# mLSTM heads of block 1: another form of the norm, gate rows spread by a transfer, and the output product cut into pieces between the heads

## What is computed

```python
att = moba_attention(q_a, k_a, v_a)                      # 8 heads of 64, causal
m_t = jnp.maximum(m_inter, jnp.max(d, axis=-1))          # mLSTM, 4 heads, q and k 64 wide, v 128
s = jnp.einsum('bhtd,bhsd->bhts', qc, kc) * jnp.exp(d - m_t[..., None])
...
h = num / jnp.maximum(jnp.abs(den), jnp.exp(-m_t))[..., None]
...
hm = hm * lax.rsqrt(jnp.mean(hm * hm, axis=-1, keepdims=True) + EPS)
hm = hm.transpose(0, 2, 1, 3).reshape(B, S, ML_V_W) * g_mlstm_out.astype(jnp.float32)
hm = hm * jax.nn.sigmoid(mo.astype(jnp.float32))
mixed = jnp.concatenate([att, hm], axis=-1).astype(x.dtype)
x = x + rms_norm(mixed @ w_out, g_mix_post)
```

## Time and profile before

| | us |
|---|---|
| median of 3 runs | 1155.46 (1154.97 to 1156.65) |
| time of the profiled execution | 1161.27 |
| its span in the trace | 1159.4 |
| TensorE busy | 1118.0 (96%) |
| VectorE busy | 816.5 (70%) |
| ScalarE busy | 526.2 (45%) |

### The profile page before, as it was taken

How to read it: one execution, slowest core, us unless ns; L and a number is a source line. 1 busy time by engine, 2 the same in 40 slices (tenths; PEclk the granted TensorE clock), 3 DMA queues, 4 the chain that set the end, 5 groups by cost and what they waited for, 6 DMA issues and landing times.

```text
span 1159.4 us, 19626 instructions
## 1 busy us (share of the span) xinstructions
PE 1118.0 (96%) x8440; PEld 1055.6 (91%) x8440; DVE 816.5 (70%) x1090; ACT 526.2 (45%) x605; POOL 12.0 (1%) x26
## 2 busy tenths in 40 slices
PE   6999888999999899999999999999999999999998
PEld 5878677999999798988999999999899899999998
DVE  5865576776766599885787788768989377666442
ACT  4544444656333543553653444345355455444432
POOL 4000000000000000000000000000000000000000
PEclk9999889999999999999998999999999999999998
DMA  7533323878887164424778998965443275676540
GB/s 211 182 121 135 108 79 105 326 267 297 315 285 252 38 218 153 138 74 158 259 257 288 319 313 294 326 213 168 166 146 110 82 261 183 204 252 202 179 165 37
DMA packets 131494, 228.61 MB, mean 197 GB/s; under 512 B 5925, under 2 KB 59539, under 8 KB 131409
## 3 DMA queue, kind: packets, MB, share of 16 engines
q1 hardware_dynamic: 130404, 227.11, 58.1%
q0 software_dynamic: 672, 0.06, 0.1%
q10 hardware_dynamic: 333, 0.21, 0.1%
HBM read 226.30 MB, written 1.05 MB: 196 GB/s over the span
## 4 chain that ended last, share of the span: by engine, by line
PE 73%; DVE 17%; ACT 6%; issue 2%; DMA 2%; SPq 0%; DVEq 0%; ACTq 0%
PE mm L422 62%; DVE lo L1117 5%; DVE cacc L1197 4%; ACT hi L799 3%; PE mm L461 2%; PE pv L479 2%; DMA raw<-in_w_out_dram 1%; PE pa L506 1%; DVE ada_acc L1138 1%; DVE sB L1205 1%; PE pv L521 1%; PE pa L501 1%; PE pv L706 1%; DMA raw<-in_w_ffn_in_dram 1%; DVE pB L1496 1%
## 5 line engine op out<-in xcount | busy, mean ns | idle before, releaser
L422 PE MATMUL mm<-act_hi,hi 128*128 128x256 f32 x1760 | 493.0, 284 | 6.0 <-ACT act_hi L861 2.7
L422 PE MATMUL mm<-act_hi,lo 128*128 128x256 f32 x1760 | 486.6, 280 | 0.0
L1117 DVE TENSOR_TENSOR lo<-raw,hi 128x2048 fp32r<-128x2048 f32 (+1 forms) x160 | 361.9, 2265 | 173.6 <-ACT hi L799 172.2
L422 PE MATMUL mm<-act_lo,hi 128*128 128x256 f32 x1760 | 470.1, 280 | 0.0
L799 ACT ACTIVATE hi<-raw 128x2048 fp32r<-128x2048 f32 (+1 forms) x160 | 301.5, 1889 | 226.7 <-PE mm L422 180.5
L422 PEld LDWEIGHTS mm<-act_hi,hi 128*128 128x128 f32 x1760 | 332.5, 189 | 11.8 <-issue 9.5
L422 PEld LDWEIGHTS mm<-act_hi,lo 128*128 128x128 f32 x1760 | 332.9, 189 | 0.8 <-issue 0.7
L422 PEld LDWEIGHTS mm<-act_lo,hi 128*128 128x128 f32 x1760 | 322.4, 189 | 0.0
L422 PE MATMUL mm<-u_hi,hi 128*128 128x256 f32 x608 | 170.7, 281 | 0.0
L422 PE MATMUL mm<-u_lo,hi 128*128 128x256 f32 x608 | 170.4, 280 | 0.0
L422 PE MATMUL mm<-u_hi,lo 128*128 128x256 f32 x608 | 169.2, 278 | 0.0
(11 more groups left out here) (247 smaller groups left out, 995.1 us busy)
## 6 DMA issues: line engine op xcount, KB each, us to landing
ada_raw<-in_ada_w_dram SPq DMA_DIRECT2D x96, 512.0 KB, 6.0
raw<-in_w_ffn_in_dram SPq DMA_DIRECT2D x88, 512.0 KB, 6.0
raw<-in_w_in_dram SPq DMA_DIRECT2D x40, 1024.0 KB, 5.1
raw<-in_w_ffn_out_dram SPq DMA_DIRECT2D x20, 1024.0 KB, 6.0
raw<-in_w_up_dram SPq DMA_DIRECT2D x16, 1024.0 KB, 6.6
raw<-in_w_down_dram SPq DMA_DIRECT2D x16, 1024.0 KB, 7.8
raw<-in_w_out_dram SPq DMA_DIRECT2D x12, 1024.0 KB, 5.1
raw<-in_w_in_dram SPq DMA_DIRECT2D x16, 512.0 KB, 5.3
```

The source lines that it names most:

```text
L422: ins = pe.matmul(o, w[:, kk, fs], a[:, k, :], start=(k == 0 and i == 0 and f % 2 == 0), stop=(ends and i == len(pairs) - 1), skip_group_c ...
L1117: v(dve.tensor_tensor(lo[:, c % RING, 0:nk, :], raw[:, c % RING, 0:nk, :], hi[:, c % RING, 0:nk, :].bitcast(F32), ALU.subtract), "lo_done")
```

## The change

It has these parts:

- `gate_rows` limits the row of the exponent to at most 41. The rows are then written to a buffer in DRAM by one transfer that ScalarE issues in unit 1, and read back, with 128 copies of each row, by four that it issues in unit 2. `bcA` has room for four heads. The spreading product L626 and the copy L934 go.
- The mask is added (0 or -1e30) before the exponential, in the instructions of `m_args`; the multiplication with the mask (L1355) goes. There are buffers `sM` and `pM` of the heads' own.
- The division goes. The norm of numerator/d equals numerator · (mean(numerator²) + eps · d²)^-1/2. ScalarE squares numerator and denominator and copies the numerator (`m_sums_out`); `emA` is exp(2·row); VectorE takes the larger of the two squares (`m_larger`) and adds eps·128 times it to the sum of squares (`m_total`); ScalarE makes the root from that (`m_root`).
- The transposes of the gates go to unit 3, the arguments of heads 0 and 1 to units 5 and 6, and unit 8, which only drained, is written out.
- The output product is cut by input tile, 12 matmuls a piece (`out_pieces`), and the pieces stand between the last units and the heads.
- ScalarE loads the table with exp and tanh after the softplus and the one with ln at the first root.

```diff
@@ TensorE
-            for i in range(UNITS + 1):
+            for i in range(UNITS):
...
                 if i + 1 < UNITS:
                     scores(qk1, i + 1)
-                if i < UNITS:
-                    turn(pA[:, i % 2, :])
+                else:
+                    out_pieces(0, (0, 1))
+                    for g in (3, 4):
+                        pe.wait_ge(sem(freed(("in", g))[0]), freed(("in", g))[1])
+                    m_scores(0)
+                turn(pA[:, i % 2, :])
...
-                full(pe.matmul(bank(1)[:], ident[0:4, h:h + 1].to_broadcast([4, P]), gate[:, 2:4, :], start=True, stop=True), 1)
...
-            m_scores(0)
-            for h in range(MH + 1):
+            out_pieces(1, (0,))
+            u = UNITS - 1
+            apply_v(ptA[:, u % 2, :], v1, u * QK, QK, QK * (u % 2), True)
+            out_pieces(0, (2,))
+            for h, (half, ks) in enumerate(((1, (1,)), (0, (3,)), (1, (2,)), (1, (3,)))):
+                m_sums(h)
                 if h + 1 < MH:
                     m_scores(h + 1)
-                if h < MH:
-                    m_sums(h)
-                if h in fill_at:
-                    chunk(("out", fill_at[h]), 0, att_hi, att_lo, ready=None if fill_at[h] else "act_ready")
-                if h:
-                    head_squares()
-
-            for half in range(2):
-                chunk(("out", half), 1, act_hi, act_lo, ready=None if half else "act_ready")
+                out_pieces(half, ks)
+                head_squares()
+                squares_at.append(filled.seen("a"))
+            out_pieces(0, (4, 5, 6, 7))
+            chunk(("out", 1), 1, act_hi, act_lo)
@@ ScalarE
+            def m_exps(h):
+
+                wait("mexp_arg_ready")
+                a(act.activation(sM[:, h % 2, :], sM[:, h % 2, :], ACT.Exp))
+                a(act.activation(emA[:, h % 2, :], bcA[:, h, S:2 * S], ACT.Exp, scale=2.0), "mexp_done")
+
+            def m_sums_out(h):
...
+                a(act.activation(sq[:, 0, :], b[:, 0:S], ACT.Square), "hsq_ready")
+                a(act.activation(bcA[:, h, 0:S], b[:, S:2 * S], ACT.Square), "den_ready")
+                if h >= 2:
+                    act.wait_ge(sem("of_ready"), MH + h - 1)
+                a(act.activation(hmA[:, h % 2, :], b[:, 0:S], ACT.Copy), "bank2_free", sums_at[h])
+
+            def m_root(h):
+
+                log_tables()
+                wait("head_sum_ready")
...
+                if i == 1:
+                    wait("gate_rows_ready")
+                    act.dma_start(gate_rows_dram[:, :], gate[:, 2:4, :].rearrange("h r s -> h (r s)")).then_inc(sem("gates_out"), 16)
+                if i == 2:
+                    act.wait_ge(sem("gates_out"), 16)
+                    for h in range(MH):
+                        act.dma_start(bcA[:, h, :], gate_rows_dram[h].partition_broadcast(P)).then_inc(sem("gates_spread"), 16)
...
+            for h in range(MH):
+                m_sums_out(h)
+                if h:
+                    m_high(h - 1)
+                m_root(h)
+                if h + 2 < MH:
+                    m_exps(h + 2)
+                if h == 2:
+                    split(groups[("out", 1)][1][0] + LEAD)
@@ VectorE
+            def m_args(h):
...
+                dve.wait_ge(sem("gates_spread"), 16 * MH)
+                v(dve.scalar_tensor_tensor(out=sM[:, i, 0:S], in0=b[:, 0:S], scalar=acol[:, 0, h:h + 1], in1=cst[:, C_UP:C_UP + S],
+                                           op0=ALU.add, op1=ALU.add))
...
-                link(dve.tensor_tensor(d, b[:, S:2 * S], emA[:, i, :], ALU.max))
-                link(dve.scalar_tensor_tensor(out=d, in0=b[:, S:2 * S], scalar=-1.0, in1=d, op0=ALU.mult, op1=ALU.max))
-                link(dve.reciprocal(d, d))
-                link(dve.tensor_tensor(hmA[:, i, :], b[:, 0:S], d, ALU.mult), "bank2_free")
...
+            for h in range(MH):
+                m_larger(h)
+                if h + 1 < MH:
+                    m_weights(h + 1)
+                if h:
+                    m_final(h - 1)
+                m_total(h)
+                if h:
+                    m_low(h - 1)
+                if h + 2 < MH:
+                    m_args(h + 2)
+            m_final(MH - 1)
+            m_low(MH - 1)
+            split(groups[("out", 1)][1][0] + LEAD)
```

More of the change, by code:

```diff
@@ L87, in constants @@
     c[:, C_ADD + 2 * P:C_ADD + 3 * P] = tri
[L88 to L91, removed]
+    up = np.where(i[:, None] <= i[None, :], 0.0, -1e30)
+    c[:, C_UP:C_UP + P] = up
+    c[:, C_UP + 2 * P:C_UP + 3 * P] = up
     return c
@@ L642, in m_sums, with out_pieces @@
                 full(pe.matmul(b[:, S + P:2 * S], ones, w[:, S:3 * P], start=False, stop=True, skip_group_check=True), 2)
-            m_scores(0)
-            for h in range(MH + 1):
+                sums_at.append(filled.seen(2))
+            def out_pieces(half, ks):
+                name = ("out", half)
+                g, ids = groups[name]
+                for k in ks:
+                    j, kk = divmod(k, CK)
+                    if kk == 0:
+                        begin(name, j)
+                    if half == 0:
+                        wait("act_ready")
+                    ins = tile_products(2 * (g % 2), ids[j] % RING, kk, k, range(GT), ((att_hi, att_lo), (act_hi, act_lo))[j], k == KD - 1)
+                    if kk == CK - 1:
+                        ins.then_inc(sem("mm_done"), 1)
@@ new lines, in _ @@
+            for i in range(UNITS):
+                if i < len(todoA):
+                    name, j = todoA[i]
+                    chunk(name, j, act_hi, act_lo, token_major=name in (("in", 2), ("in", 4)))
+                if i + 1 < UNITS:
+                    scores(qk1, i + 1)
+                else:
[4 more added lines that the diff above has]
+                turn(pA[:, i % 2, :])
+                u = i - 1
+                if u == 0:
+                    pe.wait_ge(sem(freed(("in", 2))[0]), freed(("in", 2))[1])
+                if u >= 0:
+                    apply_v(ptA[:, u % 2, :], v1, u * QK, QK, QK * (u % 2), u % 2 == 1)
+                if i == 3:
+                    wait("gate_rows_ready")
+                    b = bank(0)
+                    for tt in range(TT):
+                        ins = pe.transpose(b[:, 4 * tt:4 * tt + 4], gate[:, 5, tt * P:tt * P + P], ident[0:4, 0:4])
+                    full(ins, 0)
@@ new lines, in m_weights, with m_larger @@
+            def m_weights(h):
+                i = h % 2
+                wait("mexp_done")
+                link(dve.scalar_tensor_tensor(out=pM[:, i, :], in0=full(0)[:, 0:3 * P], scalar=SCALE, in1=sM[:, i, :],
+                                              op0=ALU.mult, op1=ALU.mult), "bank0_free")
+                dve.sem_inc(sem("mweights_ready"), 1)
+            def m_larger(h):
+                i = h % 2
+                wait("den_ready")
+                link(dve.tensor_tensor(emA[:, i, :], emA[:, i, :], bcA[:, h, 0:S], ALU.max))
@@ L1328, in _, with m_low, take_heads @@
+            def m_low(h):
+                low(hf[:, h % 2, :], act_hi[:, 4 + h, :], act_lo[:, 4 + h, :], "act_hi_ready", "act_ready")
+                v.settle()
+            def take_heads(h):
+                v(dve.tensor_copy(hf[:, h % 2, :], full(2)[:, 0:S]), "bank2_free")
+                v.settle()
+                dve.sem_inc(sem("of_ready"), 1)
+            for i in range(UNITS):
+                probs(i, pA)
                 if i == 0:
@@ L1334, in _ @@
                     softmax_max(i + 1, sA)
+                if i == 3:
+                    link(dve.tensor_copy(acol[:].rearrange("p t h -> p (t h)"), full(0)[:, 0:8]), "bank0_free")
                 if i % 2 == 1 and i >= 3:
                     low_of_heads(i // 2 - 1)
+                if i == 5:
+                    m_args(0)
+                if i == 6:
+                    m_args(1)
                 if i >= 2 and i % 2 == 0:
[L1338 to L1339 removed]
@@ L1382, in _ @@
-            m_args(0)
-            m_weights(0)
-            for h in range(MH + 1):
-                if h in fill_at:
-                    split(groups[("out", fill_at[h])][1][0] + LEAD)
+                    take_heads(i // 2 - 1)
+            m_weights(0)
+            take_heads(MH - 1)
+            split(groups[("out", 0)][1][0] + LEAD)
+            low_of_heads(MH - 1)
+            for h in range(MH):
+                m_larger(h)
                 if h + 1 < MH:
-                    m_args(h + 1)
```

139 lines of the change are left out of this document (53 added, 86 removed).

## The result

The changed kernel takes **1141.32 us** (median of 4 runs, 1138.15 to 1143.9); the kernel before, timed beside it, takes 1155.22 (4 runs, 1154.02 to 1156.65). The ratio is 0.9887, with a 95% interval of 0.9867 to 0.9908: faster by 13.9 us, where 13.8 was forecast. A second pair, taken later, gave 1140.65 beside 1156.46, ratio 0.9868 [0.9854, 0.9883], 15.8 us.

The account below looks back on a forecast made before the run. TensorE bounds the rest (954.07 of 969.90 us busy); waits and slow clock cost the stage. 115.7 + 39.9 + 5.4 = 161.0 (walk 161.2) against 175.01; 13.8 off the 1155.46 median gives 1141.7 us, range 1137.0 to 1148.0.

Parts of the forecast that it names:

- The forecast point: Start of the norm's sums of squares on TensorE: 161.2 us by the walk, against 175.01 before, 13.8 less.
- the stage: The stretch the change touches, from the end of the last input chunk to the norm; 59.55 us before.
- the 115.7: End of the attention units' input chunks, where the changed stretch starts: 115.7 us, 0.25 later than before.
- its sign of being right: Norm's sums of squares starting at 160 to 163 us of the trace, among other signs such as clock mostly 1.00.
- TensorE's work: TensorE's instructions in the changed stretch at full clock, without waits: 39.9 us; four removed spreading products 4.5 us.
- The waits: TensorE waiting for head 3, its squares, its piece, the last chunk and the norm: 0.9, 1.6, 0.7, 0.8, 1.4 us.
- the handovers of 0.1 us: Assumed delay when one engine releases another: about 0.1 us; 0 or 0.15 each moves the walk by 0.8.
- The 0.25 us: Later end of the units, from gate transposes in unit 3 waiting for VectorE: 0.25 us, bounds 0 and 1.4.
- the near bound: Landing time for the spread gate rows' transfers: 5.0 us for 1 MB; the far bound was 11.6 for 384.5 KB.
- Rival 3: Spread rows land late, VectorE waits in unit 5; about 5 us slack, then one for one, up to 1161.5; 5%.
- Rival 1: Clock still falls in part of the changed stretch, costing 1 to 6 us: 1143 to 1148, say 1145; 16%.
- The table load: ScalarE's ln table load before head 0's root: 1.28 us by the trace; the skill's 2.66 would save 0.2 less.

Follow-up runs that it names:

- the repeat: The changed kernel run once more, nothing altered: 1140.65 us beside 1156.46 for the kernel before, ratio 0.9868.
- The early split: Changed kernel with ScalarE's `hi` and VectorE's `lo` of the output product's fourth chunk made earlier, the addition before the norm not moved: 1137.03 us, ratio 0.9845.
- whole chunks: Changed kernel with the first half of the output product in two whole chunks instead of pieces: 1145.79 us, ratio 0.9921.
- the late spread: Changed kernel with the four transfers that spread the gate rows issued in unit 5 instead of unit 2: 1143.85 us, ratio 0.9895.

## Why the prediction was right

**The forecast point.** 161.2 was forecast, 160.40 came. Two errors stand behind this that partly cancel: the stage starts 1.0 later than the 115.7 taken, which the repeat shows to be no effect of the change (115.08 there), and it takes 43.7 instead of 45.5. In the repeat the point is at 158.76, outside the 160 to 163 that the prediction gave as its sign of being right, so meeting it here to 0.8 was in part luck.

**TensorE's work.** 43.68 less the four marked waits of 4.03 is 39.65, against 39.9. Its parts were less exact. A turn takes 4.20 instead of 4.59: sums 1.40 instead of 1.66 and squares 0.43 instead of 0.63, while a piece costs 1.52 and not 1.45. The sums and squares were read from a place of the earlier trace rows where they followed and preceded other instructions, and a distance to the next start belongs to both neighbours. Over the stage the differences cancel; nobody should count on that. The spreading products were taken at 1.12, the length of one, where the distance to the next instruction is 1.05: 4.2 us for the four and not 4.5. The forecast point doesn't rest on this.

**The waits.** Forecast 0.9, 1.6, 0.7, 0.8 and 1.4, together 5.4. Found in the same places and with the same releasers 0.68, 1.41, about 0.3 (a gap at 150.87 that the trace doesn't mark as a wait), 0.66 and 1.28. Each is a little smaller, so the answers came a little earlier than by the handovers of 0.1 us; which handover was too long I haven't sorted out. This is the term that was mis-sized, by 1.4 us with the unmarked gap left out. The early split confirms the reading of two of them: with the `hi` gone from ahead of the last squares, the 1.41 goes.

**Ahead of the stage.** The 0.25 us came, but not as the wait that was forecast: from the scores of unit 1 to those of unit 7, the last, it is 46.80 us, where it was 46.59 before, and the transposes in unit 3 take 0.22 with no wait in front of them. The spread rows cost nothing, as taken. A transfer of 256 KB landed in 6.2 us, where the near bound was 5.0 for 1 MB, and the four had some 16 us to spare (95 to 111). They are copies out of 8 KB, not out of 16 as the prediction says, and the four issues took 1.8 us of ScalarE's queue and not 1.3. Rival 3 was priced rightly: the slack is 5.2 where 5 was said, but beyond it the cost was not one for one in the traced execution: 2.25 us of waiting cost 5.09, with the clock (3.2 by the medians).

**The clock.** Rival 1 didn't come in the change. It came in the trace of each experiment that took the dense pieces away or made the waits longer: whole chunks, the division back, the late spread. That it was a live risk and not a remote one is shown by the two executions that part at 121.24.

**The table load.** ScalarE waited until 132.80 for VectorE, longer than a load of 1.28 from 130.35 asks. By the 2.66 us that the Trainium skill (ScalarE: Activation LUTs, What ACT_TABLE_LOAD costs) gives for a switch, it could not have gone on before 133.01; here it went on 2.45 after the load's start. With the 1.29 of the earlier trace rows this speaks for the trace's figure, though the load was covered either way.

**From trace to median.** The stage gives 15.87 us, the point 14.6, the medians 13.9 and, in the second pair, 15.8. That 13.8 met the first to 0.1 is luck within the scatter. By the stage, with 0.2 for the transposes ahead of it, the saving is 15.7, some 2 us larger than forecast; but this rests on the one trace of before, an execution that took longer than all 35 timed runs, so how much of the 2 us is real stays open.

| part put back, or alone | stage, us | against the change |
|---|---|---|
| nothing (the change, twice) | 43.68 | |
| one spreading product in the stage, three ahead of it | 44.72 | +1.04 (4.2 in all) |
| whole chunks | 46.04 | +2.36, with 4.3 more if the clock falls at 121.24 |
| late spread | 48.77 | +5.09 |
| division | 50.60 | +6.92 |
| division and whole chunks | 54.76 | +11.08, of which 4.3 where the clock fell |
| the kernel before (one trace) | 59.55 | +15.87 |

## What to carry to other kernels

Where an engine waits for a chain through two others, cut the dearest link, and put dense work of the bound engine in small pieces into what remains: in the traces here that covered the waits and held the clock, and the second could be worth more than the first (4.3 us against 2.4). Then ask of each wait that is left what stands ahead of its releaser in that engine's order; here a 1.90 us instruction moved by half a turn, and an addition moved by one split, gave 3 us more. Compare stages between two marks of the trace, not spans: where the clock held the stage repeated to 0.1 us, while the rest of the span moved by some microseconds.

## What was not expected

- **The clock can fall or hold after the same instructions at the same times** (121.24, above): 4.3 us between two executions, on two chips, with the same 0.96 and 0.79 us waits ahead.
- **It held under longer waits than those after which it fell elsewhere.** With the division back it was 1.00 from 145 to 150 us, with TensorE busy 3.43 of 5 us between waits of 2.16 and 2.52, and with dense pieces in each turn, and fell only behind 150; with whole chunks it was 0.66 right after waits of 0.40 and 0.69 among small matmuls only.
- **DMA issues from ScalarE's queue ran beside its activations.** The four issues took 0.36 to 0.52 us each on the queue, 1.8 together, and ScalarE stood idle for 0.57 around them.
